# Powers and inverse products of the RWKV-7 recurrence on four quadrants, with P + I made by GpSimd

## What is computed

```python
def rwkv7_scan(r, decay, k, v, a_vec, b_vec):
    '''S_t = S_{t-1} diag(w_t) + (S_{t-1} a_t) b_t^T + v_t k_t^T, y_t = S_t r_t.'''
    def step(state, xs):
        r_t, w_t, k_t, v_t, a_t, b_t = xs
        sa = jnp.einsum('bhvk,bhk->bhv', state, a_t)
        state = (state * w_t[:, :, None, :] + sa[..., None] * b_t[:, :, None, :]
                 + v_t[..., None] * k_t[:, :, None, :])
        return state, jnp.einsum('bhvk,bhk->bhv', state, r_t)

# mlstm_chunkwise, 4 heads: within a chunk
s = jnp.einsum('bhcld,bhcsd->bhcls', q, k) * w_intra
num = jnp.einsum('bhcls,bhcsv->bhclv', s, v) + ...
h = num / jnp.maximum(jnp.abs(den), jnp.exp(-m_row))[..., None]
```

## Time and profile before

| | |
|---|---|
| runs, median | 2821.59 us |
| the profiled execution, first to last instruction | 2818.6 us |
| busy: TensorE matmuls | 2765.8 us (98%) |
| busy: VectorE | 1955.9 us (69%) |
| busy: ScalarE | 1384.3 us (49%) |
| busy: GpSimd | 58.2 us (2%) |

### The profile page before, as it was taken

How to read it: one execution, slowest core, us unless ns; L and a number is a source line. 1 busy time by engine, 2 the same in 40 slices (tenths; PEclk the granted TensorE clock), 3 DMA queues, 4 the chain that set the end, 5 groups by cost and what they waited for, 6 DMA issues and landing times. The chain is left out here.

```text
span 2818.6 us, 48303 instructions
## 1 busy us (share of the span) xinstructions
PE 2765.8 (98%) x19892; PEld 2464.4 (87%) x19892; DVE 1955.9 (69%) x2715; ACT 1384.3 (49%) x2115; POOL 58.2 (2%) x45
## 2 busy tenths in 40 slices
PE   8999999999999999999999999999999999999998
PEld 7999888788999888999888778999888889888887
DVE  7887855676887876887855677788774469655541
ACT  4445544554544465544544555444555366444430
POOL 1000000001000001000000000100000000000000
PEclk9999999999999999999999999999999999999999
DMA  4334311103234241334222103233432211323331
GB/s 149 106 105 172 103 48 63 37 3 120 84 106 138 101 135 53 105 105 175 69 77 68 47 3 113 75 105 106 150 104 84 75 35 34 112 80 96 97 124 53
DMA packets 71065, 254.77 MB, mean 90 GB/s; under 512 B 7672, under 2 KB 8696, under 8 KB 70848
## 3 DMA queue, kind: packets, MB, share of 16 engines
q1 hardware_dynamic: 70848, 251.70, 26.9%
HBM read 249.57 MB, written 2.10 MB: 89 GB/s over the span
## 5 line engine op out<-in xcount | busy, mean ns | idle before, releaser
L261 PE MATMUL ps<-h_hi,w_space 128*128 128x512 f32 (+1 forms) x2624 | 697.2, 351 | 3.4 <-DVE h_lo L359 3.4
L271 PE MATMUL ps<-w_space 128*128 128x512 f32 x2448 | 567.3, 390 | 1.3 <-PEq L91 0.8
L271 PEld LDWEIGHTS ps<-w_space 128*128 128x128 f32 x2448 | 457.4, 188 | 96.1 <-issue 1.2
L261 PEld LDWEIGHTS ps<-h_hi,w_space 128*128 128x128 f32 x2624 | 462.4, 190 | 69.4 <-DVE h_lo L359 4.2
L249 DVE TENSOR_TENSOR w_space<-w_raw,w_space 128x1024 fp32r<-128x1024 f32 x256 | 311.9, 1231 | 258.7 <-ACT w_space L241 258.4
L261 PE MATMUL ps<-h_lo,w_space 128*128 128x512 f32 (+1 forms) x1312 | 456.9, 348 | 0.0
L942 PE MATMUL ps<-h_hi,w_space 128*128 128x256 f32 x2432 | 450.8, 283 | 0.0
L942 PEld LDWEIGHTS ps<-h_hi,w_space 128*128 128x128 f32 x2432 | 385.1, 192 | 0.2
L241 ACT CAST w_space<-w_raw 128x1024 fp32r<-128x1024 f32 x256 | 264.8, 1047 | 187.9 <-PE ps L261 102.9
L942 PE MATMUL ps<-h_lo,w_space 128*128 128x256 f32 x1216 | 344.1, 283 | 0.0
L261 PEld LDWEIGHTS ps<-h_lo,w_space 128*128 128x128 f32 x1312 | 249.3, 190 | 30.3 <-issue 0.5
(11 more groups left out here) (471 smaller groups left out, 3868.6 us busy)
## 6 DMA issues: line engine op xcount, KB each, us to landing
w_raw<-in_w_ffn_in SPq DMA_DIRECT2D x176, 512.0 KB, 3.7
w_raw<-in_w_in SPq DMA_DIRECT2D x64, 512.0 KB, 3.7
w_raw<-in_w_ffn_out SPq DMA_DIRECT2D x56, 512.0 KB, 3.7
w_raw<-in_w_up SPq DMA_DIRECT2D x44, 512.0 KB, 3.7
row_blocks<-in_w_ffn_out SPq DMA_DIRECT2D x8, 2048.0 KB, 11.8
w_raw<-in_w_out SPq DMA_DIRECT2D x24, 512.0 KB, 4.1
w_raw<-in_w_down SPq DMA_DIRECT2D x22, 512.0 KB, 3.7
w_raw<-in_w_ple_gate SPq DMA_DIRECT2D x16, 512.0 KB, 4.1
```

Of the source, the lines that this page charges most:

```text
L261: m = nc.tensor.matmul(c.ps[:, bank, t], part[:, cols], moving[:, k, t], start=(opens and k == 0 and i == 0), stop=(k == KD - 1 and i == 2 ...
L271: m = nc.tensor.matmul(c.ps[:, bank + half, :], x, part[:, half * S:(half + 1) * S], start=(first and i == 0), stop=(final and i == 2), sk ...
```

## The change

The squares from the second on and the products 1 to 4 send the results of odd heads to the other half of PSUM (`changed(r, q)`), so that their matmuls go round all four quadrants; the powers, T and the new factors are laid out by head parity q and pair j. The odd heads change halves each time; the first square and the fifth product stay within their half. Power and T results of a parity share a bank (0 or 1, columns 0 to 255 and 256 to 383).

A product now multiplies P + I with T, so nothing is added afterwards: ScalarE copies the result to T (`inverse` in ScalarE's block), and VectorE's add goes. P_i + I for i = 1 to 4 is made by GpSimd from the copied power and the identity mask (`factor`), and for i = 5 by VectorE out of PSUM (`last_factor`), so ScalarE's copy of the fifth power goes too. Product i waits for the copy of power i + 1 and for the factor, and squares 3 to 5 wait for the copy of T of two before. `solve` writes to bank 7 and waits for normalise, half of `local` to bank 5, and a few waits follow from that. In TensorE's order product 1 stands behind turn, products 2 and 3 behind next_state and pairs_of_a, and square 5 ahead of outputs.

```diff
         power = st.sb("power", [P, 2, 2, 2, 2, CHUNK])
+        factor = st.sb("factor", [P, 2, 2, 2, CHUNK])
...
+        POWER_COLS, T_COLS = slice(0, 2 * P), slice(2 * P, 3 * P)
+        quadrants = [(r, q) for r in range(2) for q in range(2)]
+        changed = lambda r, q: half(r ^ q)
...
             @block.gpsimd
                 st.zero_stale()
+                pool.wait_ge(c.rec_loaded, 16 * (l + 2))
+                for t in range(NT):
+                    for i in range(1, STEPS):
+                        pool.wait_ge(power_ready, (STEPS - 1) * t + i)
+                        if t or i > 2:
+                            pool.wait_ge(t_done, STEPS * t + i - 2)
+                        nc.gpsimd.tensor_tensor(factor[:, i % 2], power[:, i % 2, :, 0], masks[:, 3, :].unsqueeze(1).unsqueeze(1)
+                                                .to_broadcast([P, 2, 2, CHUNK]), ALU.add).then_inc(factor_ready, 1)
...
                 def square(t, i):
+                    if i >= 3:
+                        pe.wait_ge(t_ready, STEPS * t + i - 2)
+                    for o in range(2 if i < STEPS else 1):
+                        for j in range(2):
+                            at = (2 * o + j) * CHUNK
+                            for r, q in quadrants:
+                                if i == 1:
+                                    low, up = (pair_t[half(r), t % 2, n, 2 * j + q, :] for n in (N_LOW, N_UP))
+                                else:
+                                    low, up = (power[half(r), (i - 1) % 2, q, n, j, :] for n in range(2))
+                                m = nc.tensor.matmul(c.ps[half(r) if i == 1 else changed(r, q), q, at:at + CHUNK], (up, low)[o],
+                                                     (low, up)[o], start=True, stop=True)
...
                 def inverse(t, i):
+                    if i < STEPS - 1:
+                        pe.wait_ge(power_ready, (STEPS - 1) * t + i + 1)
+                    else:
+                        pe.wait_ge(last_ready, t + 1)
+                    if i < STEPS:
+                        pe.wait_ge(factor_ready, (STEPS - 1) * t + i)
...
+                                                 factor[half(r), i % 2, q, j, :], T[half(r), t % 2, q, j, :], start=True, stop=True)
...
             @block.scalar
+                def inverse(t, i):
+                    act.wait_ge(t_done, STEPS * t + i)
+                    nc.scalar.copy(T[:, t % 2].rearrange("p q j n -> p q (j n)"), c.ps[:, 0:2, T_COLS]).then_inc(t_ready, 1)
...
                     powers(t, 2)
+                    inverse(t, 1)
                     if t == 0:
-                        act.wait_ge(low_turned, 1)
+                        act.wait_ge(col_turned, 2)
                         nc.scalar.activation(floor_col[:, :, :], c.ps[:, SUM_BANK, 0:NT * M_HEADS], ACT.Exp).then_inc(floored, 1)
...
             @block.vector
-                def inverse(t, i):
-                    dve.wait_ge(t_done, STEPS * t + i)
-                    if i > 1:
-                        dve.wait_ge(t_ready, STEPS * t + i - 1)
-                    nc.vector.tensor_tensor(T[:, t % 2], T[:, t % 2], by_head(quarter(T_BANK, 0)), ALU.add).then_inc(t_ready, 1)
+                def last_factor(t):
+                    dve.wait_ge(squared, STEPS * (t + 1))
+                    dve.wait_ge(t_done, STEPS * t + STEPS - 2)
+                    nc.vector.tensor_tensor(factor[:, STEPS % 2], c.ps[:, 0:2, 0:P].rearrange("p q (j n) -> p q j n", j=2),
+                                            masks[:, 3, :].unsqueeze(1).unsqueeze(1).to_broadcast([P, 2, 2, CHUNK]),
+                                            ALU.add).then_inc(last_ready, 1)
```

More of the change, by code:

```diff
@@ L2384, in a_values @@
                     m.then_inc(av_done, 1)
-                def parts(t, i):
-                    return (power[:, i % 2, 0], power[:, i % 2, 1]) if i else (pair_t[:, t % 2, N_LOW], pair_t[:, t % 2, N_UP])
                 def square(t, i):
-                    n, n_t = parts(t, i - 1)
                     if i == 1:
                         pe.wait_ge(masked, 2 * t + 1)
-                        if t:
-                            pe.wait_ge(power_ready, STEPS * t)
-                    else:
-                        pe.wait_ge(power_ready, STEPS * t + i - 1)
-                    for o, (a, b) in enumerate(((n_t, n), (n, n_t))):
-                        if o == 0 or i < STEPS:
-                            for h, j, rows in heads:
-                                for k in range(2):
-                                    at = (o * R_HEADS + h) * CHUNK
-                                    m = nc.tensor.matmul(c.ps[half(k), SQ_BANK, at:at + CHUNK], a[half(k), h, :],
-                                                         b[half(k), h, :], start=True, stop=True)
+                    else:
+                        pe.wait_ge(power_ready, (STEPS - 1) * t + i - 1)
@@ L2415, in inverse @@
                     else:
                         pe.wait_ge(t_ready, STEPS * t + i - 1)
-                    for h, j, rows in heads:
-                        for k in range(2):
-                            m = nc.tensor.matmul(c.ps[half(k), T_BANK, h * CHUNK:(h + 1) * CHUNK], parts(t, i)[0][half(k), h, :],
-                                                 T[half(k), t % 2, h, :], start=True, stop=True)
+                    for j in range(2):
+                        at = T_COLS.start + j * CHUNK
+                        for r, q in quadrants:
+                            m = nc.tensor.matmul(c.ps[changed(r, q) if i < STEPS else half(r), q, at:at + CHUNK],
+                                                 factor[half(r), i % 2, q, j, :], T[half(r), t % 2, q, j, :], start=True, stop=True)
@@ L2571, in _ @@
                     square(t, 2)
-                    inverse(t, 1)
                     if t >= 2:
@@ L2591, in _ @@
                         pairs_of_a(t + 1)
+                    inverse(t, 3)
                     scores(h, 2)
+                    square(t, 5)
                     if t:
                         outputs(t - 1)
-                    square(t, 5)
                     inverse(t, 4)
@@ L2725, in _ @@
                     powers(t, 3)
+                    inverse(t, 2)
                     weights(h, 1)
@@ L2942, in _ @@
                     weigh(h, 0)
-                    inverse(t, 2)
                     if t:
@@ L2948, in _ @@
                     weigh(h, 1)
-                    inverse(t, 3)
                     if t:
@@ L2961, in _ @@
                         sum_squares(h - 1)
-                    inverse(t, 4)
+                    last_factor(t)
                     if more:
@@ L2968, in _ @@
                         mixout.y_lo(dve, nc, 1)
-                    inverse(t, 5)
                     weigh(h, 3)
```

68 lines of the change are left out of this document (38 added, 30 removed).

## The result

| | before | changed |
|---|---|---|
| runs, median | 2820.81 us (4 runs, 2818.85 to 2822.21) | 2839.46 us (4 runs, 2835.56 to 2846.57) |
| ratio of the times | | 1.0068, 95% interval 1.0051 to 1.0085 |
| the profiled execution, first to last instruction | 2818.6 us | 2844.8 us |
| granted clock of TensorE, mean of a run | 0.996 to 0.999 in 19 runs beside the first experiments, 0.993 to 0.999 in all 74 beside the experiments | 0.991, 0.990, 0.988, 0.986 |

The changed kernel is slower, by 18.7 us. I had forecast 2823, with a range up to 2832. Its four runs already hold a hint: in the order of the clocks in the table their spans are 2833.8, 2835.7, 2839.6 and 2844.8 us. The lower the clock, the longer the run.

The account below looks back on a forecast made before the run. TensorE seemed the bound, with VectorE and ScalarE binding once products shorten. Steps -1.0, GpSimd's contention +0.8 and clock falls +2.5 gave +2.3 us: span 2820.9, median 2823.9, taken as 2823; range 2813 to 2832.

Parts of the forecast that it names:

- Three against one before: +2.5: TensorE's clock: three falls, in t=0 of both layers and one or two in t=3, cost +2.5 us; bounds -1.9 and +13.
- t=0: First step of a layer: product 2 waits for ScalarE's power 3, TensorE idle 2.9 us; loses 1.4 us at the solve.
- -1.0 + 0.8 = -0.2: Forecast without the clock: -1.0 us from the steps of two layers, +0.8 from GpSimd's contention.
- t=3: Last step of a layer, with head norms and weight splits on VectorE: gains 0.75 us.
- the walk: Instruction-by-instruction timing of step t=2 of layer 1, and of t=0, giving gains of 0.6 us and a loss of 1.4.
- Matmuls: Four quadrants halve squares 2 to 4, half square 5 and products 1 to 4: 2.6 us of TensorE a step.
- rival 3: Matmuls in the new order of square 1 and product 5 don't overlap: up to +11 us, 2833; chance 0.08.
- t=2: Steady step of layer 1: gains 0.6 us, not 2.6, with solve at +18.6 instead of +19.21.
- over 1.5 us saved give 0.2: In t=2, over 1.5 us saved in squares and products start product 4 only 0.2 earlier, since VectorE is late.
- GpSimd: Additions of 0.65 us stay hidden; contention costs VectorE 0.1 us a step (bounds 0 and 0.6), 0.8 in all.
- rival 2: The array idles more and the clock falls in each step, 1.87 us each: +13, 2835; chance 0.14.
- The span and the median: The runs' median of 2821.6 us lies 3.0 over the profiled span of 2818.6, for what lies around it.

Follow-up runs that it names:

- table_early_filled: Changed kernel with the exponential's table loaded directly behind power 2 in t=0 and constant matmuls fitted to TensorE's remaining idle time; 2818.8 us (0.9994).
- filled: Changed kernel with plain 128x128 matmuls of a constant where TensorE stood idle, at the stage's start, in t=0 and in t=3; 2825.0 us (1.0015).
- filled_t0: Changed kernel with constant matmuls at the stage's start and in t=0 only (5, 12 and 6), not in t=3; 2836.15 us (1.0052).
- filled_t3: Changed kernel with constant matmuls in t=3 only (4 ahead of product 2, 3 ahead of scores(h,1), 4 behind solve); 2831.35 us (1.0035).
- two_quadrants: Changed kernel with odd heads kept in their half, so squares 2 to 5 and products 1 to 4 use two quadrants again; 2841.07 us (1.0074).
- casts_late: table_early_filled with two ScalarE casts for later stages moved behind the copy of power 3 and fewer constant matmuls ahead of product 2; 2818.57 us (0.9989).
- before_half: Kernel before with 7 constant matmuls in t=3, squares 2 to 5 and products 1 to 4 made for each step's first chunk only; 2835.81 us.
- before_half_heads: Kernel before with 7 constant matmuls in t=3, squares 2 to 5 and products 1 to 4 made for heads 0 and 1 only; 2813.11 us (0.9961).
- before_gap: Kernel before with two more ScalarE table loads behind floor_col in t=0 of either layer, so TensorE stands idle; 2831.21 us (1.0036).

## Why the prediction was wrong

The step that failed is the clock: its number and length of falls. "Three against one before: +2.5" was seven stretches against one, up to 27.3 us long. From the steps at full clock (table_early_filled, and filled for t=0) the changed kernel's own order is worth +1.7 - 0.45 - 0.45 - 0.1 = +0.7 us a layer, 1.5 us in all, where the forecast without its clock had -1.0 + 0.8 = -0.2. The other 17 of the 18.7 us I put down to the clock. That is a remainder: the fillers took 14.2 us away, and cost some time of their own where they are longer than the wait.

Two thoughts led there. I priced a fall at 1.87 us from t=3, and took that as the price of any fall, while a stretch at half clock can last through a whole tail, in which all is TensorE's. The changed kernel's own runs give a price by time: half clock in a share x of a run lowers its mean by x/2, so 0.986 instead of 0.991 is 2 x 0.005 x 2840 = 28 us more at half clock, and these runs are 11 us apart, so 0.4 us for each us at half clock. The two profiled executions give about the same: 68 us more at half clock and 26.2 - 1.5 us, so 0.36. And I looked for new idle time only where the walk had a large wait (t=0). In t=3 I booked the shorter matmuls as a gain, while 610 to 615 with 3.58 of 5 us busy had already been the one place of the kernel before that lost its clock. Taking matmul time out of just this place had the opposite sign (filled_t0 and filled_t3, and the profile of two_quadrants, in which the longer matmuls keep the clock in t=3).

Point by point:

- **Matmuls**: right. 0.46 us from a square to what follows, 0.32 for a product. The order of square 1 and product 5 costs nothing: square 1 takes 1.06 us (1.07 before) and product 5 0.54 (0.54 before), so rival 3 was none.
- **t=2**: right in kind and nearly in size. The walk's terms put product 1 at +6.7, not +6.6 as it says (measured +6.79), and the numbers behind it 0.1 later. Forecast scores(h,1) at +10.09, product 4 at +16.2 and solve at +18.6; measured (600.85, 606.86 and 609.31 against 590.55) +10.30, +16.31 and +18.76, with the waits for ScalarE and last_factor where I had put them. The step won 0.45 us, not 0.6; t=1 0.46, not 0.55. But "over 1.5 us saved give 0.2" hid two terms: the quadrants bring about 2 us, and the new order takes about 1.5.
- **t=3**: wrong. Forecast -0.75; at full clock -0.1, since VectorE ends last there even with ScalarE's cast out of the way (casts_late), and in the changed kernel 1.5 and 3.3 us lost with the clock.
- **t=0**: the mechanism was right, 2.93 us ahead of product 2 for 2.9 forecast. The loss by waits is 1.7, not 1.4; the rest of the 5.7 and 7.9 us is the clock's.
- **GpSimd**: 0.73 for 0.65 us, never last, and VectorE's cost 1.4 us of busy time in `carried` and 0.7 in `hid`, for 0.8 in the sum; no run shows how much of it lies on the path.
- **Rivals**: rival 2 gave 2835 and named the clock, but put a fall in each step. The profile shows none in t=1 and t=2; t=3 with its tail alone took 9 to 11 us (filled_t3, filled_t0). Its 2835 was the nearest number, but by another path. Its +13, one price and one fall a step, was too small a bound for a term of 17.
- **The span and the median**: 1.8 us lie between a run's span and its time, not 3.0; the other 1.2 is that the profiled run was faster than the median. Only the name of the term was wrong: the forecast is +2.3 on the median either way.

## What to carry to other kernels

Where TensorE is the bound, look for the stretches in which it is least busy before you shorten its work there: the clock of all that follows can go with it, here 0.4 us for each us at half clock, and a few matmuls of a constant in the gap tell whether it does. A change that gives up an order of work for faster matmuls is two changes (here some 14 us either way), to be priced one by one.

## What the runs showed of the hardware

The busy share doesn't tell alone when the clock falls. In before_half the squares take the same time with half of the matmuls, the 5 us ahead show the same 4.75 us of work as the kernel before has at full clock (1618.3 to 1623.3), and yet the clock falls in t=0 of both layers for 20.5 us. First the kernel before, then before_half:

```profile
1618.30:1623.30 5.00, 4.75 (x102) 4.28 (x95) 2.58 (x5) 2.64 (x4) 0.00 (x0) 1.00 0.01 3
```

```profile
547.80:552.80 5.00, 4.75 (x100) 4.28 (x94) 2.58 (x5) 2.37 (x4) 0.00 (x0) 1.00 0.01 3
552.80:573.30 20.50, 20.50 (x225) 16.37 (x225) 9.09 (x22) 6.04 (x14) 0.00 (x0) 0.50 0.01 2
1631.40:1651.90 20.50, 20.50 (x216) 16.36 (x218) 9.14 (x23) 5.83 (x14) 0.00 (x0) 0.50 0.01 2
```

Before_half_heads has as few matmuls, is less busy, and keeps its clock at 1.00 through both stages. What sets the two apart I haven't found; in before_half all of the squares' matmuls go through one quadrant. It stays open. Nor did the same code always fall: the changed kernel's start of the stage is that of the kernel before, and only the former showed half clock there (547.5 to 550.9). In the block of full attention, which is the same in all kernels, 8 of the 17 profiles have a stretch of 3.4 or 6.8 us at half clock and 9 have none. And one of the 20 runs of the kernel before beside before_gap took 2833.9 us at a clock of 0.993, the others 2819.2 to 2824.5. So a count of falls from one profile is one sample, and the range has to leave room for longer ones.
